# Front weights in 8 KB runs, x fetched turned, and its root applied behind the products

## The chip, the cores and the metric

The kernel runs on one core of one Trainium2 chip. The metric is device time in microseconds (us), lower is better; a time given for a kernel is the median of several executions. The core has TensorE (PE; its weight loads are shown as PEld), VectorE (DVE), ScalarE (ACT), GpSimd (POOL), and SyncE (SP), which issues the transfers from the chip's memory (HBM) to the on-chip buffer (SBUF). TensorE writes its products to a small accumulator memory (PSUM, eight banks).

## The reference

One decoder block on 256 tokens of width 1024. What matters here is its beginning: x is normalised by row and multiplied by w_in; all of z, xbc, dt, q, k, v and the gates come from that one product.

```python
def rms_norm(x, g):
    xf = x.astype(jnp.float32)
    y = xf * lax.rsqrt(jnp.mean(xf * xf, axis=-1, keepdims=True) + EPS)
    return (y * g.astype(jnp.float32)).astype(x.dtype)
...
    n = rms_norm(h, g_mix[i])
    proj = n @ w_in[i]
    z = proj[..., :SPLIT_Z]
    xbc = proj[..., SPLIT_Z:SPLIT_XBC]
    dt_raw = proj[..., SPLIT_XBC:SPLIT_DT]
    ...
    gates = jax.nn.sigmoid(proj[..., SPLIT_V:])
    y_ssd = ssd_mixer(z, xbc, dt_raw, ...) @ w_ssd_out[i]
    y_sb = stick_breaking_attention(q, k, v) @ w_sb_out[i]
    merged = gates[..., :D_MODEL] * y_ssd + gates[..., D_MODEL:] * y_sb
    h = h + merged @ w_out[i]
    h = h + memory_cross_attention(rms_norm(h, g_xattn[i]), rms_norm(mem, g_mem[i]), ...)
    h = h + moe_ffn(rms_norm(h, g_moe[i]), ...)
return rms_norm(h, g_final)
```

The root of a row (the rsqrt) is one number for each token; g_mix is one number for each of the 1024 channels.

## The kernel before

**Two parts.** The front (0 to about 305 us) holds everything up to the router of the mixture of experts; behind it 32 experts follow, whose weights (`w_gu`, `w_down`, 403 MB) are streamed from HBM. All weights pass through one area, `ring`, in SBUF.

**Stripes and chunks.** The front's matrices are cut into stripes of 512 columns (`STRIPES`), and each stripe into chunks of 512 rows by 512 columns, 1 MB each (`CHUNKS`, 42 of them). Stripes 0 to 2 are xbc, then come q, k, v, two of z, four of the gates, and the later matrices. SP fetches the chunks in order into five slots of the ring (L588, a chunk as 128 partitions by four runs of 2 KB) and refills a slot when the low part of the chunk in it has been made.

**Two halves of every number.** A front product is made as three fp32r products: high weight by high x, low weight by high x, high weight by low x. ScalarE rounds a chunk to its high part (`splits_to`, L1487; the first chunk tile by tile in `first_high`, L1525). The low part is weight less high part (`low_part`, L513), four tiles of 128x512 for each chunk: VectorE makes tiles 0 and 1 of chunk 0 and all of chunk 1, GpSimd makes tiles 2 and 3 of chunk 0 and all of chunks 2 and up. There are three buffers of halves (`SPLIT`), so ScalarE can only be three chunks ahead of TensorE. The order of work is written out by hand for each engine; every hand-over is a semaphore.

**The start.** SP fetches x by rows into `h` (L575), seven rows of parameters (L578 to L581), and then the first five chunks. The squares of x are summed by ScalarE (block 0) and VectorE (block 1, L1818), GpSimd takes the root (`root`, L692 and L695), ScalarE (L1493) and VectorE (L1825) scale x, and TensorE turns it with 16 transposes (L889) into PSUM. The parameters are turned into columns `pcol` by another transpose (L902, L1833). From PSUM, x times g_mix is rounded to `xT_hi` (VectorE L1848, ScalarE L1533), and `xT_lo` is the rest (VectorE, L1842). While it waits, TensorE multiplies ones by ones (`ones_products`, L896).

**The first products.** Stripe 0 (`first_products`, L829) takes for each of its two chunks 16 products of high by high, 16 by the low x, and 16 of the low weight. From stripe 1 on (L808) TensorE goes tile by tile and waits for the low part of each tile in the first quarter of a chunk. For xbc, ScalarE applies the last tap of the convolution out of PSUM (L1553) and VectorE adds the other three (L1865); stripe n+2 writes the same banks as stripe n and waits for that. The stripes of q, k, v, z and the gates are emptied by ScalarE (`empty`, L1511), 128x1024 at a time.

**Into the experts.** SP issues the first expert weights as front buffers come free (`EARLY`, `first_free`, `pair_free`), on the same queue behind the chunks.

## Time and profile before

| | us |
|---|---|
| median of 3 runs | 1224.63 (1223.62 to 1225.7) |
| span of the profiled execution | 1222.8 |
| front: first weight product to the router's end | 11.35 to 304 |
| experts and end | 304 to 1222.8 |

The span runs from the first to the last instruction of one execution; the median stands 1.83 us above it. The page of the profile gives the busy time of each engine, the span in 40 slices, the chain of work that ended last, and the costliest groups of instructions. Other views of the trace list instructions in order of time, group them by source line, tell who waited for whom, and give the busy time of each engine in chosen stretches. TensorE's fp32 products count as two instructions in these views; one with fp32r operands as one. Ends of TensorE's instructions are modelled, so starts are read.

### The profile page before, as it was taken

Reading aid. Unit: us, or ns where it says so; the run is one execution under the profiler, and the core shown is the slowest. Engines: PE = TensorE matmul, PEld = TensorE weight load, DVE = VectorE, ACT = ScalarE, POOL = GpSimd, SP = SyncE. Lnnn points to the kernel's source line nnn. Section 1 sums busy time; section 2 is a strip of 40 time slices with the busy share of each in tenths; the row PEclk is TensorE's granted clock in tenths of the full one; section 3 lists DMA queues with packets and bytes.
Section 4 is the critical chain, followed back from the end, with each engine's and each line's share of the span. In section 5 each row is a group of like instructions: output and inputs, shape, how many; then the busy total and the mean of one; then the engine's idle time right before and its main releaser. Section 6 shows DMA issues by size and latency. Waiting matters only on the chain.

```text
span 1222.8 us, 15282 instructions
## 1 busy us (share of the span) xinstructions
PE 1161.0 (95%) x6802; PEld 591.8 (48%) x6802; DVE 302.0 (25%) x463; ACT 245.0 (20%) x349; POOL 235.6 (19%) x206
## 2 busy tenths in 40 slices
PE   9999999999999999999999999989999998899996
PEld 9998878998433333333333333333333333333332
DVE  5448363224311221121122112111211211121112
ACT  6486686445101000000000000000000000000001
POOL 6979769882001000000000000000000000000000
PEclk9999999999999999999999999999999999999999
DMA  9644537848899999999999999999999999999994
GB/s 318 209 138 140 171 104 275 318 154 366 369 426 427 421 429 426 437 430 428 429 429 431 435 431 430 428 433 431 430 430 432 429 431 434 429 429 410 428 427 199
DMA packets 44702, 451.56 MB, mean 369 GB/s; under 512 B 4916, under 2 KB 5272, under 8 KB 27736
## 3 DMA queue, kind: packets, MB, share of 16 engines
q1 hardware_dynamic: 44632, 450.54, 88.8%
q8 instruction: 55, 0.90, 0.3%
q14 instruction: 15, 0.12, 0.0%
HBM read 449.48 MB, written 1.05 MB: 368 GB/s over the span
## 4 chain that ended last, share of the span: by engine, by line
PE 62%; DMA 33%; DVE 2%; ACT 1%; issue 1%; POOL 1%; DVEq 0%; ACTq 0%; POOLq 0%
DMA ring<-in_w_down 20%; PE ps L1275 19%; PE ps L1299 12%; PE ps L865 10%; DMA spare_quad<-in_w_down 7%; DMA kv_quad<-in_w_down 6%; PE ps L808 6%; PE ps L1246 3%; PE ps L1321 2%; PE ps L1178 2%; PE ps L829 1%; PE ps L1312 1%; PE ps L1197 1%; PE ps L980 1%; PE ps L889 0%
## 5 line engine op out<-in xcount | busy, mean ns | idle before, releaser
L513 POOL TENSOR_TENSOR w_parts<-ring,w_parts 128x512 fp32r<-128x512 f32 x162 | 216.9, 1373 | 42.0 <-ACT w_parts L1487 33.3
L692 POOL TENSOR_SCALAR ss<-ss 128x1 f32<-128x1 f32 (+2 forms) x8 | 1.5, 191 | 868.9 <-ACT junk L1477 864.5
L1275 PE MATMUL ps<-ring,xs 128*64 128x512 f32 x688 | 151.8, 595 | 5.8 <-DMA ring<-in_w_gu 5.8
L2216 DVE TENSOR_SCALAR xbuf<-ps 128x512 f32<-128x512 f32 x32 | 22.1, 691 | 526.4 <-PE ps L1275 526.4
L1299 PE MATMUL ps<-ring,xbuf 128*64 128x512 f32 x576 | 128.1, 595 | 17.0 <-DMA ring<-in_w_down 17.0
L1275 PE MATMUL ps<-ring,nT 128*64 128x512 f32 x560 | 123.5, 595 | 3.6 <-DMA ring<-in_w_gu 3.6
L1747 ACT ACTIVATE xbuf<-xbuf 128x512 f32<-128x512 f32 x32 | 20.2, 631 | 469.0 <-DVE xbuf L2216 469.0
L865 PE MATMUL ps<-w_parts,xT_hi 128*128 128x512 f32 x352 | 110.4, 395 | 0.0
L1275 PEld LDWEIGHTS ps<-ring,xs 128*64 128x64 f32 x688 | 47.9, 137 | 101.5 <-issue 90.3
L1487 ACT ACTIVATE w_parts<-ring 128x2048 fp32r<-128x2048 f32 x41 | 78.2, 1915 | 65.3 <-PE ps L865 39.4
L1299 PEld LDWEIGHTS ps<-ring,xbuf 128*64 128x64 f32 x576 | 43.9, 137 | 90.0 <-issue 85.2
L1757 ACT ACTIVATE xbuf<-ps 128x512 f32<-128x512 f32 x31 | 18.5, 597 | 336.5 <-PE ps L1321 336.5
L1275 PEld LDWEIGHTS ps<-ring,nT 128*64 128x64 f32 x560 | 39.2, 137 | 81.0 <-issue 73.9
L865 PEld LDWEIGHTS ps<-w_parts,xT_hi 128*128 128x128 f32 x352 | 65.3, 188 | 14.4 <-issue 0.9
L865 PE MATMUL ps<-w_parts,xT_lo 128*128 128x512 f32 x176 | 68.7, 390 | 0.0
L2232 DVE COPY xbuf<-ps 128x512 f32<-128x512 f32 x32 | 22.1, 691 | 167.7 <-PE ps L1299 167.7
L1246 PE MATMUL ps<-xbuf,scr 64*128 64x512 f32 x248 | 61.6, 615 | 0.8 <-DVE xbuf L2232 0.8
L808 PE MATMUL ps<-xT_hi,w_parts 128*128 128x256 f32 x320 | 57.9, 284 | 0.0
L1299 PE MATMUL ps<-spare_quad,xbuf 128*64 128x512 f32 x224 | 49.9, 595 | 6.7 <-DMA spare_quad<-in_w_down 6.7
L1275 PE MATMUL ps<-spare_quad,nT 128*64 128x512 f32 x240 | 53.2, 595 | 1.8 <-DMA spare_quad<-in_w_gu 1.8
L1275 PE MATMUL ps<-kv_quad,nT 128*64 128x512 f32 x224 | 49.7, 594 | 1.8 <-DMA kv_quad<-in_w_gu 1.8
L808 PEld LDWEIGHTS ps<-xT_hi,w_parts 128*128 128x128 f32 x320 | 49.9, 192 | 0.0
(312 smaller groups left out, 1314.3 us busy)
## 6 DMA issues: line engine op xcount, KB each, us to landing
ring<-in_w_gu SPq DMA_DIRECT2D x24, 4096.0 KB, 41.5
ring<-in_w_gu SPq DMA_DIRECT2D x30, 2048.0 KB, 14.8
ring<-in_w_down SPq DMA_DIRECT2D x12, 4096.0 KB, 39.7
spare_quad<-in_w_gu SPq DMA_DIRECT2D x8, 4096.0 KB, 41.5
kv_quad<-in_w_gu SPq DMA_DIRECT2D x8, 4096.0 KB, 41.6
ring<-in_w_in SPq DMA_DIRECT2D x24, 1024.0 KB, 5.2
ring<-in_w_down SPq DMA_DIRECT2D x12, 2048.0 KB, 14.7
kv_quad<-in_w_gu SPq DMA_DIRECT2D x10, 2048.0 KB, 15.0
```

The lines of the kernel that those rows point to most:

```text
L513: ops.tensor_tensor(w_lo[:, m % SPLIT, c], ring_slot(m)[:, c], w_hi[:, m % SPLIT, c], ALU.subtract).then_inc(lo_ready[name], 1)
L808: i = mm(ps[:, b0 + cb // 2, (cb % 2) * T:(cb % 2 + 1) * T], w[:, k, cb * P:(cb + 1) * P], a[:, 4 * c + k, :], start=(c == 0 and k == 0 an ...
L865: i = mm(ps[:, b0 + b, :], a[:, 4 * c + k, b * P:(b + 1) * P], w[:, k, :], start=(c == 0 and k == 0 and q == 0), stop=(4 * c + k == STRIPE ...
L1178: mm(ps[64 * half:64 * half + 64, 4 + q, :], sel[quadrant(i), e, :], bgu[quadrant(i), :], start=True, stop=False, skip_group_check=True)
L1246: i = mm(ps[:, 2 * b + half, :], hot[r, b, :], yb[r, :], start=False, stop=False, skip_group_check=True)
L1275: i = mm(ps[64 * half:64 * half + 64, 4 + q, :], xg[:, k, (j % GE) * SLOTS:(j % GE + 1) * SLOTS], w[:, q * FF + half * 512:q * FF + half * ...
L1299: i = mm(ps[64 * half:64 * half + 64, 6, :], turned[:, k, :], w[:, k % 4, half * 512:(half + 1) * 512], start=(k == 0), stop=(k == FF // P ...
L1321: i = mm(ps[r, 7, c * 64:(c + 1) * 64], actv[r, c * 64:(c + 1) * 64], ident[r, r], start=True, stop=True)
L1487: af(w_hi[:, m % SPLIT, :], ring_slot(m), ACT.Copy).then_inc(hi_ready, 1)
L1747: af(sg, gl, ACT.Sigmoid, scale=ALPHA).then_inc(sg_ready, 1)
L2216: V.tensor_scalar(gl, ps[:, 4, :], LIM, None, ALU.min).then_inc(gl_ready, 1)
L2232: return V.tensor_copy(yb, ps[:, 6, :])
```

## The change

The host lays the inputs out anew (only copies and transposes, no arithmetic): every chunk lies as 128 rows of 8 KB, one for each partition; x comes twice, by rows and turned (channels on partitions, two halves of 4 KB runs); the parameter columns come ready. On the chip:

- x is not scaled or turned. ScalarE and VectorE round turned x times g_mix out of SBUF (`x_high`, `x_low`), and the products are of x without its root.
- The row copy of x is fetched eighth, behind chunk 2. Its squares are summed as before, ScalarE takes a square root (`root`), VectorE the reciprocal.
- TensorE makes the row of roots behind stripe 0 (`scale_row`): the column of roots, repeated, by the identity, so that each partition holds the root of all 256 tokens. VectorE copies it (`x_scale`).
- VectorE multiplies the xbc stripes in PSUM by that row before ScalarE's tap (`scale_stripe`), and empties q and k with it in place of ScalarE. v, z and the gates are scaled as ScalarE empties them, now in two instructions of 128x512. The step's 16 columns are scaled where their bias is added.
- The halves of `w_dt` are made later, behind stripe 1's taps; GpSimd's product for the router stands a little later.

```diff
-WARM = (18, 8, 4)
+WARM = (20, 4)
...
+            sp_.dma_start(pcol[:], columns).then_inc(prm_in, 16)
+            fetch_x(0)
             for m, (n, c) in enumerate(CHUNKS):
...
+                if m == 0:
+                    half = LO_HALF * SW
+                    halves = chunks[m].rearrange("(a q) (s n) -> a (q s) n", a=2, s=2)
+                    sp_.dma_start(ring_slot(m)[:, 0:half], halves[0]).then_inc(first_in, 16)
+                    sp_.dma_start(ring_slot(m)[:, half:], halves[1]).then_inc(slot_full[slot(m)], 16)
+                    fetch_x(1)
+                else:
+                    sp_.dma_start(ring_slot(m), chunks[m]).then_inc(slot_full[slot(m)], 16)
+                if m == 2:
+                    sp_.dma_start(h[:], x_rows).then_inc(x_in, 16)
...
+            def scale_row():
+                pe.wait_ge(consts, 5)
+                pe.wait_ge(rstd, 1)
+                for b in range(TB):
+                    i = mm(ps[:, 5, b * P:(b + 1) * P], ss[:, b:b + 1].broadcast_to([P, P]), ident[:],
+                           start=True, stop=True)
+                i.then_inc(row_done, 1)
...
             ones_products(WARM[0])
-            pe.wait_ge(prm_in, 16 * 7)
-            pe.wait_ge(consts, 5)
-            nc.tensor.transpose(ps[:, 3, 0:ROWS], prow, ident[0:ROWS, 0:ROWS]).then_inc(pt_done, 1)
-            ones_products(WARM[1])
-            pe.wait_ge(normed_act, 1)
-            pe.wait_ge(normed, NORMED[TR_X])
-            pair_transposes(xn, (0, 1, 2, 3))
-            for n in range(3):
-                stripe(n, xT, tiles=x_lo if n == 0 else None)
+            pe.wait_ge(prm_in, 16)
+            stripe(0, xT)
+            scale_row()
+            stripe(1, xT)
+            stripe(2, xT)
...
+                if name in ("v", "z", "gate"):
+                    act.wait_ge(rstd, 1)
+                    for b in range(TB):
+                        ins = af(dst[:, b], src[:, b], func, scale=ss[:, b:b + 1])
+                    return ins.then_inc(stripe_out["act"], 1)
...
+            x_high((2, 3))
             first_high((0, 1))
             first_high((2, 3))
+            x_high((4, 5, 6, 7))
             splits_to(2)
-            act.wait_ge(dtw_in, 64)
-            af(w_dt_hi[:], w_dt[:], ACT.Copy).then_inc(dt_hi, 1)
+            act.wait_ge(x_in, 16)
+            squares(h[:, 0, :], 0)
+            act.wait_ge(sq_dve, 1)
+            root(0, 2)
             for n in range(3):
                 splits_to(products_done(n) + SPLIT - 2)
                 act.wait_ge(chunk_used, products_done(n))
                 splits_to(products_done(n) + SPLIT - 1)
+                act.wait_ge(x_scaled, n + 1)
...
-            empty(FIRST["q"], scale=DH ** -0.5)
-            empty(FIRST["k"])
+            splits_to(products_done(FIRST["k"]) + SPLIT - 1)
...
+            x_low((0, 1), x_hi_dve, 0)
+            x_low((2, 3), x_hi, 2)
             low_part(dve, V, "dve", 0, tiles=range(LO_HALF))
+            x_low((4, 5, 6, 7), x_hi, 2)
             for m in range(1, LO_DVE):
                 low_part(dve, V, "dve", m)
+            dve.wait_ge(x_in, 16)
+            squares(xn, h, 0)
+            dve.wait_ge(deviation, 1)
+            V.reciprocal(ss[:, 0:2], ss[:, 0:2]).then_inc(rstd, 1)
+            dve.wait_ge(row_done, 1)
+            step(V.tensor_copy(x_scale[:], ps[:, 5, 0:T]))
...
+            def scale_stripe(n):
+                src = channel_stripe(n)
+                V.tensor_tensor(src, src, x_row, ALU.mult).then_inc(x_scaled, 1)
```

What stands in a row on TensorE at the start, before; L896 is the ones, L902 and L889 are transposes, L829 is stripe 0 and L808 stripe 1:

```order
L896 MATMUL ps<-ones 128x128 x18
L902 MATMUL ps<-ident,xbuf 128x100
L896 MATMUL ps<-ones 128x128 x8
L889 MATMUL ps<-ident,xn 128x128 x16
L829 MATMUL ps<-xT_hi,w_parts 128x256 x16
L829 MATMUL ps<-xT_lo,w_parts 128x256 x16
```

And in the changed kernel, where L899 is the ones, L832 stripe 0, L906 the row of roots and L811 stripe 1:

```order
L899 MATMUL ps<-ones 128x128 x20
L832 MATMUL ps<-xT_hi,w_parts 128x256 x16
L832 MATMUL ps<-xT_lo,w_parts 128x256 x16
L832 MATMUL ps<-xT_hi,w_parts 128x256 x32
L832 MATMUL ps<-xT_lo,w_parts 128x256 x16
L832 MATMUL ps<-xT_hi,w_parts 128x256 x16
L906 MATMUL ps<-ident,ss 128x128 x2
L811 MATMUL ps<-xT_hi,w_parts 128x256 x2
```

The transposes are gone, and the two products of the row of roots stand between stripe 0 and stripe 1.

ScalarE at the same place, before; L1477 is the squares, L1493 the scaled x, L1525 and L1487 high parts of weights, L1533 high parts of x, L1544 the half of `w_dt`, L1553 the taps of stripe 0:

```order
L1477 ACTIVATE junk,ss<-h 128x1024
L1493 ACTIVATE xn<-h,ss 128x1024
L1525 ACTIVATE w_parts<-ring 128x512 x2
L1533 ACTIVATE xT_hi<-ps,pcol 128x256 x2
L1525 ACTIVATE w_parts<-ring 128x512 x2
L1533 ACTIVATE xT_hi<-ps,pcol 128x256 x4
L1487 ACTIVATE w_parts<-ring 128x2048 x2
L1544 ACTIVATE w_dt_hi<-w_dt 128x128
L1487 ACTIVATE w_parts<-ring 128x2048 x2
L1553 ACTIVATE xcT<-ps,pcol 128x256 x4
```

And in the changed kernel, where L1549 is the high part of x, L1534 and L1495 those of weights, L1485 the squares, L1525 the square root, L1570 the taps and L1574 the half of `w_dt`:

```order
L1549 ACTIVATE xT_hi<-x_raw,pcol 128x256 x2
L1534 ACTIVATE w_parts<-ring 128x512 x4
L1549 ACTIVATE xT_hi<-x_raw,pcol 128x256 x4
L1495 ACTIVATE w_parts<-ring 128x2048 x2
L1485 ACTIVATE junk,ss<-h 128x1024
L1525 ACTIVATE ss<-ss,eps 128x2
L1495 ACTIVATE w_parts<-ring 128x2048 x2
L1570 ACTIVATE xcT<-ps,pcol 128x256 x4
L1495 ACTIVATE w_parts<-ring 128x2048 x2
L1570 ACTIVATE xcT<-ps,pcol 128x256 x4
L1574 ACTIVATE w_dt_hi<-w_dt 128x128
```

The squares moved from the front of the queue to behind the high parts of chunks 1 and 2, and `w_dt` moved behind stripe 1.

## Rows read from the trace of the kernel before

**Rows 1.** The page: busy time by engine, and GB/s in 40 slices of the span
```profile
PE 1161.0 (95%) x6802; PEld 591.8 (48%) x6802; DVE 302.0 (25%) x463; ACT 245.0 (20%) x349; POOL 235.6 (19%) x206
...
GB/s 318 209 138 140 171 104 275 318 154 366 369 426 427 421 429 426 437 430 428 429 429 431 435 431 430 428 433 431 430 430 432 429 431 434 429 429 410 428 427 199
```

**Rows 2.** Stretches: us, busy of each engine (instructions), TensorE's clock, DMA share, GB/s
```profile
310.00:320.00 10.00, 10.00 (x50) 4.68 (x49) 4.62 (x16) 0.00 (x0) 0.00 (x0) 1.00 0.72 274
...
700.00:800.00 100.00, 92.11 (x550) 35.36 (x548) 16.01 (x24) 5.38 (x11) 0.00 (x0) 1.00 1.00 430
```

**Rows 3.** Waits of PE, 12 to 350 us: us in total, times, longest
```profile
PE ps L1178 <- DVE xbuf L2217: 1.4, 1, 1.4
...
PE ps L1038 <- DVE xcT L1997: 0.6, 1, 0.6
```

**Rows 4.** Waits of SP's queue, 0 to 340 us, same columns
```profile
SPq L588 <- POOL w_parts L513: 209.0, 35, 15.2
SPq L533 <- PE ps L1275: 20.2, 4, 8.7
```

**Rows 5.** The chain, 0 to 300 us: start, us, what
```profile
14.94 8.89 PE ps L829 x72
23.83 23.04 PE ps L808 x192
...
136.28 1.01 ACT gates L1511
...
155.30 5.02 POOL w_parts L513 x4
```

**Rows 6.** TensorE in order of time, 0 to 12 us: start, us, what
```profile
1.20 6.10 PE L896 MATMUL ps<-ones 128*128 128x128 f32 x36 [1.20 <-POOL ones L699]
...
7.33 1.97 PE L896 MATMUL ps<-ones 128*128 128x128 f32 x16
...
11.35 0.84 PE L829 MATMUL ps<-xT_hi,w_parts 128*128 128x256 f32 x5
```

**Rows 7.** SP in order of time: start, us, what
```profile
0.80 0.45 SPq L575 DMA_DIRECT2D h<-in_x  x1
...
3.83 4.61 SPq L588 DMA_DIRECT2D ring<-in_w_in  x5
```

**Rows 8.** Issue to landing: x (L575), chunks 1 and 2, chunks 2 to 4 (L588)
```profile
DMA to landing us min/median/max: 5.2/5.2/5.2
...
DMA to landing us min/median/max: 7.6/8.6/9.7
...
DMA to landing us min/median/max: 9.7/11.9/14.9
```

**Rows 9.** ScalarE in order of time
```profile
12.59 1.56 ACT L1533 ACTIVATE xT_hi<-ps,pcol 128x256 fp32r<-128x256 f32 x4
14.01 3.74 ACT L1487 ACTIVATE w_parts<-ring 128x2048 fp32r<-128x2048 f32 x2
22.53 0.31 ACT L1544 ACTIVATE w_dt_hi<-w_dt 128x128 fp32r<-128x128 f32 x1 [4.78 <-DMA head_rows<-in_d_skip]
```

**Rows 10.** Line 513 in 15 to 24.5 us: ns min/median/max, first and last start
```profile
L513 DVE TENSOR_TENSOR w_parts<-ring,w_parts x3: 675/677/679, 16.8 to 18.0; 128x512 fp32r<-128x512 f32 x3
...
L513 POOL TENSOR_TENSOR w_parts<-ring,w_parts x2: 1292/1901/2510, 17.9 to 20.4; 128x512 fp32r<-128x512 f32 x2
...
L513 POOL TENSOR_TENSOR w_parts<-ring,w_parts x3: 1291/1292/1301, 20.4 to 22.9; 128x512 fp32r<-128x512 f32 x3
```

**Rows 11.** Groups by line: busy us, mean ns, idle before them
```profile
L1511 ACT ACTIVATE gates<-ps 128x1024 f32<-128x1024 f32 x4 | 4.1, 1016 | 0.0
...
L1601 ACT ACTIVATE scr<-ps 128x512 f32<-128x512 f32 x8 | 4.3, 596 | 6.7 <-PE ps L966 6.7
...
L2061 DVE TENSOR_TENSOR ps<-ps,gates 128x1024 f32<-128x1024 f32 x2 | 2.5, 1233 | 10.1 <-PE ps L865 10.1
...
L1818 DVE CUSTOM_DVE_ANT_0 xn<-h 128x1024 f32<-128x1024 f32 x1 | 1.2, 1224 | 6.0 <-DMA h<-in_x 6.0
```

More of the change, by code:

```diff
@@ L465, in build @@
         tr_done = sem("tr_done")
+        xr_in = [sem(f"xr_in{i}") for i in range(2)]
+        first_in, row_done, x_scaled = map(sem, ("first_in", "row_done", "x_scaled"))
         x_hi, x_hi_dve, x_lo, y_hi, y_lo, m_hi, m_lo, h_hi, h_lo = map(
             sem, ("x_hi", "x_hi_dve", "x_lo", "y_hi", "y_lo", "m_hi", "m_lo", "h_hi", "h_lo"))
-        table_in = sem("table_in")
-        pt_done, pcol_ready = sem("pt_done"), sem("pcol_ready")
         tap_out, conv_done, silu_done = sem("tap_out"), sem("conv_done"), sem("silu_done")
@@ L1510, in empty, with root @@
                            "gate": lambda: gates[:, :, i * SW:(i + 1) * SW]}[name]()
+                if name in ("v", "z", "gate"):
[3 more added lines that the diff above has]
+                    return ins.then_inc(stripe_out["act"], 1)
                 return af(dst, src, func, scale=scale).then_inc(stripe_out["act"], 1)
+            def root(c0, cols):
+                act.wait_ge(sq_done, sq[0])
+                s = ss[:, c0:c0 + cols]
+                af(s, s, ACT.Sqrt, bias=eps[:], scale=1.0 / D).then_inc(deviation, 1)
             act.wait_ge(consts, 4)
-            af(rsm[:, 0:4], mhalf[:], ACT.Square).then_inc(table_in, 1)
-            act.wait_ge(table_in, 1)
-            act.wait_ge(x_in, 16)
-            squares(h[:, 0, :], 0)
-            normalise(xn, h, 0, 1)
+            step(af(rsm[:, 0:1], eps[:], ACT.Sqrt, bias=eps[:], scale=1.0 / D))
             def first_high(tiles):
-                act.wait_ge(slot_full[slot(0)], filled(0))
+                act.wait_ge(*((first_in, 16) if tiles[0] < LO_HALF else (slot_full[slot(0)], filled(0))))
                 for k in tiles:
@@ L1554, in _ @@
                        scale=pcol[:, ROW_CW + 3 * NCB + c:ROW_CW + 3 * NCB + c + 1]).then_inc(tap_out, 1)
+                if n == 1:
+                    act.wait_ge(dtw_in, 64)
+                    af(w_dt_hi[:], w_dt[:], ACT.Copy).then_inc(dt_hi, 1)
             act.wait_ge(dt_chan, 1)
@@ L1882, in per_head @@
                 return head_rows[:, i, :].unsqueeze(1).broadcast_to([P, TB, H_SSD])
-            V.tensor_tensor(dt4[:, 0], ps[:, 4, 0:32].rearrange("p (b h) -> p b h", b=TB), per_head(0),
-                            ALU.add).then_inc(dt_raw, 1)
+            for b in range(TB):
+                i = V.scalar_tensor_tensor(out=dt4[:, 0, b], in0=ps[:, 4, b * H_SSD:(b + 1) * H_SSD],
+                                           scalar=ss[:, b:b + 1], in1=head_rows[:, 0, :], op0=ALU.mult, op1=ALU.add)
+            i.then_inc(dt_raw, 1)
             dve.wait_ge(dt_raw, 1)
@@ L2287, in _, with laid_out, by_partition @@
                                        op0=ALU.mult, op1=ALU.mult).then_inc(out_ready, 1)
-_INS = ["x", "mem", "g_mix", "w_in", "conv_w", "conv_b", "dt_bias", "a_log", "d_skip", "g_ssd", "w_ssd_out",
-        "w_sb_out", "w_out", "g_xattn", "g_mem", "w_xq", "w_xkv", "w_xo", "g_moe", "w_router", "b_router",
-        "w_gu", "b_gu", "w_down", "b_down", "g_final"]
+_INS = ["x_rows", "x_turned", "columns", "mem_rows", "chunks", "w_step", "dt_bias", "a_log", "d_skip", "g_moe",
+        "w_router", "b_router", "w_gu", "b_gu", "w_down", "b_down"]
+def laid_out(inputs):
+    def by_partition(rows):
+        return np.asarray(rows).reshape(-1, P, rows.shape[-1]).transpose(1, 0, 2)
+    a = dict(inputs)
+    a["x_rows"], a["mem_rows"] = by_partition(inputs["x"][0]), by_partition(inputs["mem"][0])
+    a["x_turned"] = by_partition(np.asarray(inputs["x"])[0].T).reshape(P, 2, KD // 2, T).transpose(1, 0, 2, 3)
+    rows = [np.asarray(inputs[n]).reshape(-1, P) for n in ("g_mix", "g_xattn", "g_mem", "g_ssd", "conv_w", "conv_b",
+                                                           "g_final")]
+    a["columns"] = np.concatenate(rows).T
+    a["w_step"] = by_partition(np.asarray(inputs["w_in"])[0, :, COL_DT:COL_Q])
+    chunks = []
+    for n, c in CHUNKS:
+        _, mat, col, _, _, _ = STRIPES[n]
+        chunks.append(by_partition(np.asarray(inputs[mat])[0, c * 4 * P:(c + 1) * 4 * P, col:col + SW]).reshape(P, CH))
+    a["chunks"] = np.stack(chunks)
+    a["chunks"][0] = chunks[0].reshape(P, 2, CH // 2).transpose(1, 0, 2).reshape(P, CH)
+    return a
 def kernel(**inputs):
```

124 lines of the change are left out of this document (59 added, 65 removed).

## The prediction

> **What bounds the kernel now.** First the page: TensorE is busy 95% of the span, and GB/s stands near 430 in nearly every slice from the twelfth on [rows 1]. So there are two parts. From about 340 us on, the weights of the experts run without a gap (a DMA share of 1.00 and 430 GB/s in 700 to 800 us, TensorE idle for 8 us in it [rows 2]): the end is the moment at which this stream began, plus its bytes at 430 GB/s. It began when buffers came free, and SP waited for that: 20.2 us in four waits for TensorE [rows 4]; between 310 and 320 us the share is only 0.72 [rows 2]. So an advance of TensorE in the front should move the whole stream forward, one for one.
>
> In the front TensorE is the bound. Its waits between 12 and 350 us that are longest are 1.4 and 0.6 us [rows 3]; the chain runs along its products, 192 of them in 23.04 us, 0.12 us each [rows 5]. The chunks are not late: SP stood 209 us in 35 waits for a slot to come free [rows 4]. What is open is the start, 11.35 us until the first weight product [rows 6], and whatever new wait comes behind it.
>
> **The start.** Before, the first products wait for x, its root, its scaling and the transposes. Now they wait for the ones, turned x, its rounding, and the first half of chunk 0. Ones: 18 products (36 instructions) begin at 1.20 and the next batch at 7.33, 8 products in 1.97 us, 0.25 each [rows 6]. Twenty end at 7.3 + 2 x 0.25 = 7.8. Stripe 0 is 96 products of 0.12, 11.5 us, to 19.3 if nothing is late; the row of roots is two fp32 products of 128 columns like the ones, 0.5 us, to 19.8. Stripe 1 began at 23.83 [rows 5], so this path alone would gain 4.0 us.
>
> **The transfers.** x by rows landed 5.2 us after its issue at 0.80, at 6.0 [rows 7, 8]. The five chunks were issued from 3.83 on, some 0.5 us apart; chunk 1 (at 4.3) landed at 11.9, chunk 2 (4.8) at 14.5, so 1 MB takes about 2.6 us there. In the new order chunk 2 is again the end of the fourth megabyte, behind two halves of x, two of chunk 0, and chunk 1: no later than 14.5 at the old rate. At the rate of the expert stream, 430 GB/s [rows 2], a megabyte takes 2.44 us and it lands at 6.0 + 3 x 2.44 = 13.3, the other bound. I take 13.9, between them, since its runs are 4 and 8 KB, neither the 2 KB of before nor the longer ones of the experts. By the same ladder (2.5 us for 1 MB): turned x first half 5.0, chunk 0 in halves 6.3 and 7.6, x second half 8.9, chunk 1 11.4, x by rows 16.4, chunk 3 18.9, chunk 4 21.4.
>
> **What rides on them.** ScalarE: a tile of x takes 0.39 us (1.56 for four), a chunk's high part 1.87 (3.74 for two) [rows 9]. The first two high tiles of chunk 0 are there by 7.7, in time for TensorE at 7.8; x tiles 4 to 7 at 10.5; chunk 1 at 13.3, needed at 13.6; chunk 2 at 13.9 + 1.9 = 15.8. VectorE's part of chunk 1 is four times 0.68 [rows 10], done at 16.1, needed from 17.6. So stripe 0 runs nearly without a stop.
>
> GpSimd is the tight one. It may begin chunk 2 at 15.8, four tiles at 1.29 us; but one of before took 2.51, the one that began at 17.9 while VectorE was at its own line 513 (until 18.6 + 0.7) [rows 10]. VectorE's squares, 1.22 us [rows 11], read two SBUF operands and fall at 16.4 to 17.6, so I charge half of that collision: 5.2 + 0.6, and GpSimd ends at 21.7 (21.1 without, 22.3 with all of it). TensorE wants the fourth tile of chunk 2 nine products into stripe 1, at 19.8 + 1.1 = 20.9. It stops for 0.8 us. Stripe 1 then ends 87 products later, at 21.7 + 10.4 = 32.1. Before, it ended at 23.83 + 11.52 = 35.35. **Gain 3.25 us.** From chunk 3 on GpSimd makes a chunk in 5.2 us and TensorE uses one in 5.76, and ScalarE no longer stands 4.78 us for the small transfers behind `w_dt` [rows 9]; there the distance grows again.
>
> The Trainium skill speaks against this change here: SBUF — State Buffer, section "Who interferes with whom", says that GpSimd shares a pair of SBUF ports with VectorE under an exclusive lock. The trace agrees with the 2.51 us tile; by the rule alone, with all squares inside GpSimd's chunk, the gain would be 0.6 us less, without it 0.6 more. The low parts of x, now read from SBUF and not PSUM, fall under it as well, but before 12.4 us, when GpSimd has only two tiles to make.
>
> **The root.** x by rows lands at 16.4; squares 1.2, square root and reciprocal some 0.2 each with their hand-overs: the root is there at about 18.3, before TensorE asks at 19.3. Everything on TensorE is queued behind that wait, so each microsecond that the row copy comes after 17.4 is lost whole.
>
> **The scaling.** VectorE gets three products of 128x1024 on PSUM, 1.23 us each (taken from line 2061, which does the same [rows 11]). For stripes 1 and 2 they run while ScalarE makes a high part (1.87), ahead of its taps, and cost nothing; if ScalarE had no such part first, each would cost its 1.23. For stripe 0 they end at 21.5, before ScalarE has made chunk 4 (lands 21.4, 23.3); its convolution ends near 30, and stripe 2 wants that bank at 32.1. q and k leave ScalarE (2 x 1.0) for VectorE, which waits there anyway.
>
> v, z and the gates are emptied by two instructions of 0.60 in place of one of 1.02 [rows 11], 0.2 us more, up to 0.3 with the scale. Seven times, but ScalarE is ahead of TensorE at most of them. Only in the stick-breaking part does a chain pass through it: gates at 136.28, then GpSimd's chunk at 155.30 [rows 5], and at its end TensorE waits 0.6 us on line 1038 [rows 3]. There I charge 0.3 us, between 0 and 0.6 (two of them).
>
> **Sum.** 3.25 - 0.3 = 2.95 us, and the chunks' faster landing later in the front is worth nothing, since slots and not transfers are waited for. The span goes from 1222.8 to 1219.9; the median stands 1.83 above the span, so 1224.63 - 2.95 = 1221.7.
>
> **The rivals.**
>
> *GpSimd in time.* Chunk 2 lands at 13.3 and VectorE's squares miss GpSimd's tiles: 13.3 + 1.9 + 5.3 = 20.5, no stop. Gain 4.0, to 1220.6. For it speaks the stream's rate with long runs; against it that the first transfers start cold.
>
> *Inputs at the old rate.* The longer runs don't speed the first transfers. Chunk 2 at 14.5 and a full collision: 14.5 + 1.9 + 6.4 = 22.8, stripe 1 ends at 33.2, 2.1 gained, 0.3 to 0.6 lost: 1222.9. The row copy would land at 17.1, still in time. This is also the case in which the new layout does nothing.
>
> *The gain stays in the front.* The experts' stream sets its own time from 340 us on; if its start hung on transfers and not on TensorE, the end would stay: 1224.6. For it: 8% of TensorE idle there [rows 2]. Against it: SP's waits for TensorE and the share of 0.72.
>
> *Slower: each transfer pays its fixed time.* The first four megabytes are now eight transfers with the small one, not five. x took 5.2 us, of which 1 MB at 430 GB/s is 2.44, so 2.8 are fixed. If the three added ones paid this in turn, chunk 2 would land 8 us later, stripe 1 end at 40, and the kernel take about 1224.6 - 2.95 + 8 = 1229.7. The point is 1 us each (3 us in all use up the gain). Against it: the chunks issued 0.5 us apart land some 2.6 us apart with 7.6 to 9.7 from issue to landing [rows 8], so they overlap.
>
> **How the numbers follow.** Forecast 47% (1221.7, its own range 1221.0 to 1222.5), GpSimd in time 16% (1220.6), old rate 22% (1222.9), gain left in the front 8% (1224.6), slower 7% (1226 and more). About 0.2%, 2.4 us, is what can be told from no change, so faster is under 1222.2: most of the first, all of the second, a little of the third, 0.57. Same: 0.35; slower: 0.08. The range takes in the best case less half the spread of the runs before (2.1 us), 1219.6, and the old rate and most of the fourth case above: 1224.6.
>
> **What would show it.** Right: first weight product near 7.8, row of roots without a wait near 19.3, stripe 1 from 19.8 with a stop of 0.8 us for GpSimd's line, stripe 2 from about 32.1, the last router product some 3 us before that of now, and the same 430 GB/s behind it. Wrong: a wait of TensorE for the root, a stop inside stripe 0 for chunk 1's high part (it has 0.3 us to spare), a stop of stripe 2 for the convolution, or an expert stream at another rate: 0.3% of 900 us would undo the gain.

## The result and the profile after

The changed kernel takes 1232.03 us (median of 5 executions, 1230.91 to 1233.82), the kernel before, beside it, 1224.09. The ratio is 1.0062, 95% interval [1.0051, 1.0073]: slower by 7.9 us, where 2.9 us less were forecast. The profiled execution is the slowest of its five; its span is 1232.0, 9.2 us above the 1222.8 of before, and the accounts below are made against that one.

The page of the changed kernel, busy time by engine and GB/s in 40 slices, to be read against [rows 1]:

```profile
PE 1163.9 (94%) x6777; PEld 591.0 (48%) x6777; DVE 315.3 (26%) x469; ACT 246.6 (20%) x355; POOL 235.5 (19%) x205
...
GB/s 339 218 100 140 192 115 214 306 172 315 382 430 424 425 427 428 431 431 434 426 434 431 428 434 430 429 431 430 432 429 430 435 427 434 431 425 414 427 427 187
```

The stream of the experts has the rate it had. VectorE has gained 13 us of busy time, far more than the three products of 1.23 us, and the emptying of q and k, that it got. TensorE's waits (us in total, times, longest), 5 to 400 us, show one that is not in [rows 3]:

```profile
PE ps L922 <- POOL identx L725: 8.6, 1, 8.6
...
PE ps L1046 <- DVE xcT L2042: 0.6, 1, 0.6
PE ps L811 <- POOL w_parts L512: 0.6, 1, 0.6
```

Line 922 is the 24 products of `w_dt`. The view names GpSimd's copies to `identx`. They raise a counter (`consts`) that those products wait for too, but the products want 9 of it, and GpSimd has made its ninth before its first tile. What they also wait for is `dt_lo`, the low half of `w_dt`, and that is VectorE's. VectorE in order of time (start, us, what), 40 to 54 us:

```profile
39.73 2.43 DVE L1903 SCALAR_TENSOR_TENSOR xcT<-ps,pcol,xcT 128x254 f32<-128x254 f32 x5
42.07 11.30 DVE L1917 TENSOR_TENSOR w_dt_lo<-w_dt,w_dt_hi 128x128 fp32r<-128x128 f32 x1
53.29 1.22 DVE L1893 TENSOR_TENSOR ps<-ps,x_scale 128x1024 f32<-128x1024 f32 x1
```

GpSimd in the same order, 14 to 54 us:

```profile
16.65 6.01 POOL L512 TENSOR_TENSOR w_parts<-ring,w_parts 128x512 fp32r<-128x512 f32 x4 [4.36 <-ACT w_parts L1495]
23.22 29.95 POOL L512 TENSOR_TENSOR w_parts<-ring,w_parts 128x512 fp32r<-128x512 f32 x24 [0.55 <-ACT w_parts L1495]
53.12 0.39 POOL L725 COPY identx<-ident 32x128 f32<-32x128 f32 x1
```

A subtraction of 128x128 stands in the records as 11.30 us of work on VectorE. It asked at 42.07 and ended at 53.37, 0.2 us after the end of GpSimd's run of 24 tiles without a gap (53.17). GpSimd did not stand still there: its next instruction, a copy, began at 53.12. TensorE was ready for the products at 44.9, 1.9 us ahead of before (46.87, the two chain rows of [rows 5]), and began at 53.5. It then lost a second time. Stretches of the changed kernel (us, busy time of PE, PEld, DVE, ACT, POOL with instructions, granted clock, DMA share, GB/s):

```profile
44.00:46.00 2.00, 0.94 (x8) 0.73 (x7) 2.00 (x1) 0.98 (x1) 2.00 (x3) 1.00 0.69 209
46.00:48.00 2.00, 0.00 (x0) 0.00 (x0) 2.00 (x1) 0.93 (x1) 2.00 (x2) 1.00 0.75 315
48.00:50.00 2.00, 0.00 (x0) 0.00 (x0) 2.00 (x1) 0.00 (x0) 2.00 (x3) 0.59 0.49 70
50.00:52.00 2.00, 0.00 (x0) 0.00 (x0) 2.00 (x1) 0.00 (x0) 2.00 (x3) 0.50 0.93 393
52.00:57.00 5.00, 3.49 (x17) 2.40 (x18) 3.84 (x5) 1.93 (x4) 4.20 (x12) 0.50 0.59 208
57.00:59.00 2.00, 2.00 (x13) 1.51 (x12) 1.89 (x6) 0.20 (x1) 0.00 (x0) 0.60 0.20 78
59.00:61.00 2.00, 2.00 (x20) 2.00 (x18) 1.89 (x5) 0.17 (x1) 0.00 (x0) 1.00 0.00 0
```

The granted clock fell to 0.50 (1.2 of 2.4 GHz) while TensorE stood idle and was still there when the products came. They are three groups of 8; their mean is 0.41 us in the changed kernel:

```profile
L922 PE MATMUL ps<-xT_hi,w_dt_lo 128*16 128x256 f32 x8 | 3.3, 415 | 0.0
L922 PE MATMUL ps<-xT_lo,w_dt_hi 128*16 128x256 f32 x8 | 3.3, 411 | 0.0
L922 PE MATMUL ps<-xT_hi,w_dt_hi 128*16 128x256 f32 x8 | 3.3, 410 | 8.6 <-POOL identx L725 8.6
```

and 0.276 in the kernel before:

```profile
L914 PE MATMUL ps<-xT_hi,w_dt_hi 128*16 128x256 f32 x8 | 2.2, 276 | 0.0
```

From the first of them to the next stripe that makes 5.2 us against 2.7. The account: 1.9 us ahead at 44.9, 8.6 lost in the wait, 2.5 in the clock, so 9.2 behind (64.74 against 55.57 at the second half of the q stripe). The span ends 9.2 behind too, but that the two are equal is chance: on the way 0.3 us are lost at the gates, 1.2 regained at 300 to 310 us, where the clock fell in the kernel before and not here, and 1.0 lost again behind 340 us.

### The profile page after: what moved, and what is told of

It reads as the page before. It is cut to its first block, busy times and chain, and to the rows that moved or that the text cites. A ratio compares the mean times of both kernels' runs of the same rounds, so it can differ in the third digit from the quotient of the medians.

```text
span 1232.0 us, 15241 instructions
## 1 busy us (share of the span) xinstructions
PE 1163.9 (94%) x6777; PEld 591.0 (48%) x6777; DVE 315.3 (26%) x469; ACT 246.6 (20%) x355; POOL 235.5 (19%) x205
## 4 chain that ended last, share of the span: by engine, by line
PE 59%; DMA 34%; POOL 3%; DVE 2%; ACT 1%; issue 1%; SPq 0%; DVEq 0%; ACTq 0%; POOLq 0%
PE ps L1283 19%; DMA ring<-in_w_down 16%; PE ps L1307 12%; PE ps L868 10%; DMA spare_quad<-in_w_down 6%; DMA kv_quad<-in_w_down 6%; PE ps L811 4%; DMA kv_quad<-in_w_gu 3%; PE ps L1254 3%; POOL w_parts L512 3%; PE ps L1329 2%; PE ps L1186 2%; DMA ring<-in_chunks 1%; PE ps L1205 1%; PE ps L1320 1%
## 5 line engine op out<-in xcount | busy, mean ns | idle before, releaser
L1495 ACT ACTIVATE w_parts<-ring 128x2048 fp32r<-128x2048 f32 x41 | 78.4, 1915 | 68.4 <-PE ps L868 39.2
L811 PE MATMUL ps<-xT_hi,w_parts 128*128 128x256 f32 x320 | 58.3, 284 | 0.6 <-POOL w_parts L512 0.6
L811 PEld LDWEIGHTS ps<-xT_hi,w_parts 128*128 128x128 f32 x320 | 49.9, 192 | 1.1 <-POOL w_parts L512 0.8
```

Source lines behind the costliest of these rows:

```text
L811: i = mm(ps[:, b0 + cb // 2, (cb % 2) * T:(cb % 2 + 1) * T], w[:, k, cb * P:(cb + 1) * P], a[:, 4 * c + k, :], start=(c == 0 and k == 0 an ...
L1495: af(w_hi[:, m % SPLIT, :], ring_slot(m), ACT.Copy).then_inc(hi_ready, 1)
```

## The experiments

### Which instruction: four runs

**Theory L**: the low half of `w_dt` on VectorE, with both operands in SBUF, gets no turn while GpSimd's line 512 runs on. The first run takes it off VectorE; its edit to the changed kernel:

```diff
             for m in range(LO_DVE, 9):
                 low_part(pool, nc.gpsimd, "pool", m)
+                if m == 5:
+                    pool.wait_ge(dtw_in, 64)
+                    pool.wait_ge(dt_hi, 1)
+                    nc.gpsimd.tensor_tensor(w_dt_lo[:], w_dt[:], w_dt_hi[:], ALU.subtract).then_inc(dt_lo, 1)
...
-                if c == 7:
-                    dve.wait_ge(dt_hi, 1)
-                    V.tensor_tensor(w_dt_lo[:], w_dt[:], w_dt_hi[:], ALU.subtract).then_inc(dt_lo, 1)
```

> The changed kernel, but the low half of w_dt is made by GpSimd itself, behind the low part of chunk 5, not by VectorE. Theory L (VectorE's instruction with two SBUF operands gets no turn while GpSimd's line 512 runs without a gap, 42.1 to 53.4 us): the 8.6 us wait of TensorE goes, and with it the 2.5 us that its first 24 products behind it took longer at the lower clock; TensorE reaches the w_dt products near 45 us, the time is 1221 to 1223. Rival W (w_dt or its high half lands late): the wait stays, 1232. Rival S (the scaling by VectorE is what costs): 1229 to 1232.

Measured: 1221.60 us against 1224.45, ratio 0.9977 [0.9967, 0.9987], the first version faster than before. GpSimd makes the half in 0.47 us, and TensorE reaches the products at 44.91 without a wait. By tile (ns, start):

```profile
L724 POOL TENSOR_TENSOR w_dt_lo<-w_dt,w_dt_hi x1: 473/473/473, 37.8 to 37.8; 128x128 fp32r<-128x128 f32 x1
```

The second leaves it on VectorE and has GpSimd stop for it:

```diff
+                if m == 7:
+                    pool.wait_ge(dt_lo, 1)
                 low_part(pool, nc.gpsimd, "pool", m)
```

> The changed kernel with one wait added: GpSimd waits for the low half of w_dt before it begins the low part of chunk 7. VectorE's instruction, its place and its operands are as in the changed kernel. Theory L: it ends when GpSimd ends chunk 6 (about 43.5 us), busy for some 1.5 us and not 11.3, and the time is 1221 to 1223. If the instruction is slow for a reason of its own or waits for its data, it still ends near 53 us, GpSimd waits with it, and the time is 1232 or more.

Measured: 1222.20 us, ratio 0.9985 [0.9975, 0.9994]; the half took 0.80 us:

```profile
41.95 0.80 DVE L1919 TENSOR_TENSOR w_dt_lo<-w_dt,w_dt_hi 128x128 fp32r<-128x128 f32 x1
```

The third gives the kernel before nothing but this one move (ScalarE's high half behind stripe 1's taps, VectorE's low half behind its convolution):

```diff
-            dve.wait_ge(dt_hi, 1)
-            V.tensor_tensor(w_dt_lo[:], w_dt[:], w_dt_hi[:], ALU.subtract).then_inc(dt_lo, 1)
...
+                if c == 7:
+                    dve.wait_ge(dt_hi, 1)
+                    V.tensor_tensor(w_dt_lo[:], w_dt[:], w_dt_hi[:], ALU.subtract).then_inc(dt_lo, 1)
```

> The kernel before with this one part of the change: both halves of w_dt are made behind stripe 1's taps and convolutions, nothing else is changed. Theory L: VectorE's instruction begins near 44 us and ends when GpSimd's run ends at 55; TensorE, which asks at 46.9, waits 8 us, and loses up to 2.5 more at the lower clock: 1232 to 1235. If the wait belongs to the new start (scaling, late transfers), this kernel takes 1224.

Measured: 1233.99 us, ratio 1.0083 [1.0066, 1.01]. VectorE there:

```profile
43.88 10.79 DVE L1878 TENSOR_TENSOR w_dt_lo<-w_dt,w_dt_hi 128x128 fp32r<-128x128 f32 x1
```

The fourth puts a copy of `w_dt` into an unused bank of PSUM (ScalarE) and subtracts from there, so that VectorE reads one operand from SBUF; GpSimd runs on:

```diff
+                    af(ps[:, 7, 0:P], w_dt[:].rearrange("p k n -> p (k n)"), ACT.Copy).then_inc(dt_hi, 1)
...
-                    dve.wait_ge(dt_hi, 1)
-                    V.tensor_tensor(w_dt_lo[:], w_dt[:], w_dt_hi[:], ALU.subtract).then_inc(dt_lo, 1)
+                    dve.wait_ge(dt_hi, 2)
+                    V.tensor_tensor(w_dt_lo[:], ps[:, 7, 0:P].rearrange("p (k n) -> p k n", k=KD), w_dt_hi[:],
+                                    ALU.subtract).then_inc(dt_lo, 1)
```

> The changed kernel, but ScalarE also copies w_dt to a free PSUM bank and VectorE takes the first operand from there; order and place stay. Theory L (it is the second SBUF operand that needs GpSimd's turn): the instruction takes some 0.2 to 0.3 us beside GpSimd's run, as the convolution's do (0.48 us for 128x253, one operand in PSUM), and the time is 1221 to 1223. If any VectorE instruction that reads SBUF is held: 11 us and 1232.

Measured: 1222.53 us, ratio 0.9984 [0.9974, 0.9994]:

```profile
42.03 0.28 DVE L1918 TENSOR_TENSOR w_dt_lo<-ps,w_dt_hi 128x128 fp32r<-128x128 f32 x1
```

At the same place and time it takes 0.28 us instead of 11.30. Theory L holds, and the move of this one step carries the whole loss: alone it costs the kernel before 9.5 us, and the change without it is no slower than before.

### The dose, and the clock

GpSimd's pause one chunk later than in the second run (ahead of chunk 8, not 7):

> The changed kernel, with GpSimd waiting for the low half of w_dt ahead of its chunk 8 instead of not at all (the run before paused it ahead of chunk 7 and came to 1222.2). Theory (the low half ends where GpSimd first pauses, wherever that is): it ends at about 48.2, takes some 6 us where it took 11.3 without a pause and 0.80 with the earlier one, TensorE waits some 3.5 us, and the time lies between the two, 1225 to 1227. Rival (the low half is slow for a reason of its own, such as its place in VectorE's row, and the earlier run was quick because GpSimd's chunk 7 came later): it still takes 10 us or more and ends near 53, time 1230 or more.

Measured: 1227.37 us, ratio 1.0025 [1.0014, 1.0035], a little above the range expected; TensorE waited 3.1 us, and the half ended at 48.16, just behind the end of GpSimd's last tile before the pause (48.0):

```profile
42.37 5.79 DVE L1919 TENSOR_TENSOR w_dt_lo<-w_dt,w_dt_hi 128x128 fp32r<-128x128 f32 x1
```

For the clock, TensorE was given products of ones to do in the wait, first 24, then 36 (`ones_products(24, 6)` behind `stripe(2, xT)`):

> The changed kernel, with 24 more products of ones on TensorE behind stripe 2, in the wait for the low half of w_dt; nothing else differs. Theory (the wait is set by VectorE's low half, which gets no turn until GpSimd's run of line 512 ends, and the wait then costs a second time because TensorE's granted clock fell to 0.50 in it): the low half still takes some 11 us and ends at about 53, the ones fill some 6 of the 8.6 us, the 24 products of w_dt take 2.7 us where the changed kernel took 5.24, and the time is 2.5 us less than the changed kernel's 1232.0, about 1229.5. Rival (the clock is no cause, and what came after the wait was late for another reason): the 24 products still take about 5 us, time about 1232.

> The changed kernel with 36 products of ones behind stripe 2 (the run before had 24, and left TensorE idle for 2.6 us). Theory (the fall of the granted clock is the second half of the loss, and an idle stretch of 2.6 us still brought it on): the ones at 0.23 us each fill the whole wait, from about 44.9 to 53.2, the granted clock stays 1.00, the 24 products of w_dt take 2.7 us (5.24 in the changed kernel, 4.35 in the run with 24), time about 1229.5. Rival (the products of w_dt are slow for another reason than the idle time): they still take more than 4 us, time 1231 or more.

With 24 they ended at 50.2, TensorE stood idle for the 2.6 us that were left, and the clock fell all the same; the products took 4.35 us, a miss of the expectation:

```profile
52.00:57.00 5.00, 4.22 (x23) 2.98 (x24) 3.81 (x7) 1.93 (x4) 3.45 (x12) 0.66 0.65 210
```

With 36 there was no idle time and the products took 2.73 us (53.10 to 55.83):

```profile
52.00:57.00 5.00, 5.00 (x45) 4.43 (x44) 3.84 (x6) 2.27 (x5) 3.80 (x12) 1.00 0.59 215
```

So the traces show the 2.5 us to be the clock's. The medians don't resolve it: 1231.43 with 24 and 1230.92 with 36 (4 executions each), 0.6 and 1.1 us under the changed kernel, with intervals of the ratios that overlap; about 1229.5 was expected of both. In the profiled execution with 36 TensorE is 2.8 us ahead of the changed kernel at the second half of q, but only 0.8 at 340 us: at 310 to 320 us its granted clock was 0.69, and 1.00 in the changed kernel.

### The other parts of the change

Long runs alone: the kernel before, its chunks laid out by the host as in the change.

```diff
-                src = mats[mat][c * 4 * P:(c + 1) * 4 * P, col:col + SW]
-                sp_.dma_start(ring_slot(m).rearrange("p (k n) -> p k n", k=4),
-                              src.rearrange("(k p) n -> p k n", p=P)).then_inc(slot_full[slot(m)], 16)
+                sp_.dma_start(ring_slot(m), chunks[m]).then_inc(slot_full[slot(m)], 16)
```

> The kernel before, with only the front's weights laid out in 8 KB runs; x and its root, the order of VectorE, ScalarE and TensorE and the row of roots stay as they were. Theory (the front's transfers are not what the path waits for once the first chunks are in): the time stays within 1.5 us of the kernel before, 1223 to 1225, though the small packets fall to about a fifth. Rival (long runs bring the chunks earlier and the path follows): the first stripes end 1 us or more earlier, and the time is 1222.5 or less. Second rival (the long runs come later, as chunks 3 and 4 did in the changed kernel): 1226 or more.

Measured: 1224.13 us against 1224.46, ratio 1.0001 [0.9992, 1.001]. Packets under 8 KB fall from 27736 to 6232, and nothing follows, as the prediction had it: slots are waited for.

GpSimd's late begin on chunk 2: the first version of above, with four tiles of 128x512 on ScalarE in place of one instruction of 128x2048 for that chunk.

```diff
+                    if m == 2:
+                        for k in range(KT):
+                            c = slice(k * SW, (k + 1) * SW)
+                            af(w_hi[:, m % SPLIT, c], ring_slot(m)[:, c], ACT.Copy).then_inc(hi_ready, 1)
```

> The changed kernel with the low half of w_dt made by GpSimd behind its chunk 5 (the run that came to 1221.6), and with ScalarE rounding chunk 2 in four tiles of 128x512 instead of two of 128x1024, so that GpSimd can begin on the first of them earlier. Theory (stripe 1's stop of about 0.6 us and what follows it is set by GpSimd's late begin on chunk 2): GpSimd begins 0.8 to 1.3 us earlier, the stop goes, and the time falls by 0.3 to 1.0 us below that run, to 1220.6 to 1221.3. Rival (ScalarE's four instructions cost more than the two, and what is gained at chunk 2 is lost at chunks 3 and 4): 1221.6 or more.

Measured: 1221.19 us, ratio 0.9977 [0.9968, 0.9986]: inside the range expected, but not to be told from the 0.9977 without. GpSimd began 1.8 us earlier and the stop for it was gone, but VectorE's squares then took 2.31 us beside it (1.96 without), and TensorE stood for the root instead:

```profile
PE ps L912 <- DVE ss L1891: 0.5, 1, 0.5
```

### Why this instruction and no other

Elsewhere in the same traces VectorE instructions with two SBUF operands met GpSimd's line 512 and had their turn at the end of the tile. So what is special here? Three runs of the changed kernel, with one line each ahead of the low half: a wait for the end of the tap before it; a wait for the end of stripe 2; a 128x512 subtraction of two pieces of x.

```diff
+                    dve.wait_ge(conv_done, 8)
...
+                    dve.wait_ge(chunk_used, products_done(2))
...
+                    V.tensor_tensor(xn[:, 0, 0:SW], h[:, 0, 0:SW], h[:, 0, SW:2 * SW], ALU.subtract)
```

> The changed kernel, with one more wait on VectorE: the low half of w_dt starts only when the tap before it has ended (before, the two overlap by 0.08 us); GpSimd's run is left alone. Everywhere else in the traces a VectorE instruction with two SBUF operands that came upon GpSimd's line 512 got its turn at the next end of a tile, 1.3 us at most; this one alone passed nine ends. Theory B (it is passed over because it follows an instruction of another kind without a gap): it gets its turn at the next end, takes at most 1.6 us, TensorE waits not at all, time about 1222. Theory S (it is passed over for its shape, 128x128): it still takes about 11 us, time about 1232.

> The changed kernel, with VectorE waiting ahead of the low half of w_dt until TensorE has done stripe 2, so that it stands idle for over 2 us before it (the run sent beside this one gives it only the end of its predecessor); GpSimd's run is left alone. Theory B (passed over because it follows another instruction closely): it begins at about 45, has its turn at the next end of a tile, ends by 46.6, TensorE waits up to 1.7 us, time 1223 to 1225. Theory S (passed over for its shape): it begins at about 45 and ends at about 53, TensorE waits over 8 us, time about 1232.

> The changed kernel, with one more VectorE instruction, a difference of two SBUF halves of x (128x512, its result is used by nobody), between the tap and the low half of w_dt. Theory B (what follows the tap closely is passed over, whatever its shape): the added instruction takes some 11 us and the low half 0.3 us behind it, time about 1232. Theory S (the shape 128x128 is what is passed over): the added one takes at most 2 us, as others of its shape did beside GpSimd, and the low half follows within it or stalls for 9 us.

Measured: 1231.97, 1232.56 and 1232.75 us. VectorE in the first, the second and the third:

```profile
41.82 10.55 DVE L1918 TENSOR_TENSOR w_dt_lo<-w_dt,w_dt_hi 128x128 fp32r<-128x128 f32 x1
```

```profile
45.35 7.76 DVE L1918 TENSOR_TENSOR w_dt_lo<-w_dt,w_dt_hi 128x128 fp32r<-128x128 f32 x1 [2.82 <-PE ps L811]
```

```profile
42.60 11.73 DVE L1916 TENSOR_TENSOR xn<-h 128x512 f32<-128x512 f32 x1
54.26 0.37 DVE L1918 TENSOR_TENSOR w_dt_lo<-w_dt,w_dt_hi 128x128 fp32r<-128x128 f32 x1
```

Whatever came, after whatever, stood until GpSimd's run was over. Theories B (its predecessor) and S (its shape) both fall.

**Theory R**: it is how long GpSimd has run without standing still. Three more runs: two such 128x512 subtractions as probes in the version with PSUM (behind the second block of stripe 0 and of stripe 1); a pause of GpSimd ahead of chunk 5; both halves of `w_dt` one stripe earlier.

```diff
+                if c in (1, 5):
+                    V.tensor_tensor(xn[:, 0, 0:SW], h[:, 0, 0:SW], h[:, 0, SW:2 * SW], ALU.subtract)
...
+                if m == 5:
+                    pool.wait_ge(x_scaled, 2)
...
-                if c == 7:
+                if c == 3:
```

> The version with the first operand of the low half of w_dt in PSUM (1222.5 us), with two more VectorE instructions of two SBUF halves of x (128x512, results used by nobody): one behind the second block of taps of stripe 0, near 29.5 us, some 5 tiles into GpSimd's unbroken run, the other behind the second block of stripe 1, near 39, some 12 tiles in. Theory R (VectorE gets its turn early in a run of GpSimd, and no more once the run is long): the first takes at most 2 us, the second stalls until GpSimd next stands still, near 53, and the time is 1230 or more. Theory T (only the stretch behind stripe 1 is bad, for something that happens there): both take at most 2 us, time 1222 to 1224. If already the first stalls, so that the convolution comes 20 us late, neither holds, and then what matters lies before 29.5 us.

> The changed kernel, with GpSimd waiting ahead of its chunk 5 for VectorE's product over stripe 1 (34.7 us), some 1.4 us of standstill in the middle of its run; the low half of w_dt then comes upon a run of 6 tiles and not of 15. Theory R (the length of the run decides): it gets its turn at the next end of a tile and takes at most 1.6 us, TensorE does not wait for it, time 1222 to 1223.5. Theory T (the place decides): it takes about 11 us, time about 1232.

> The changed kernel, with both halves of w_dt one stripe earlier: the high one on ScalarE behind the taps of stripe 0 (27.5 us), the low one on VectorE behind the convolution of stripe 0 (32.4 us, 7 tiles into GpSimd's run). Theory R (early in a run VectorE gets its turn; elsewhere it did so 7 tiles in): the low half takes at most 1.6 us, TensorE does not wait for it, time 1222 to 1223. Theory T: the same. Theory W (in this run of GpSimd VectorE is passed over wherever it asks): it stalls from 32.4 on, the products over stripe 1 and with them the taps come some 20 us late, TensorE waits for the bank, time 1236 or more.

The probes both had their turn (1222.29 us in one execution). The second was 12 tiles into the run, where theory R said it would stand. So from here on the theory is another: a turn given to VectorE counts like a standstill, and the first probe had been given one between; the distance from that is 9.2 us.

```profile
29.49 0.69 DVE L1917 TENSOR_TENSOR xn<-h 128x512 f32<-128x512 f32 x1
...
39.33 1.36 DVE L1917 TENSOR_TENSOR xn<-h 128x512 f32<-128x512 f32 x1
```

With the early pause the low half took 0.41 us (1223.27 us, ratio 0.9992 [0.9982, 1.0002]). GpSimd and VectorE there:

```profile
34.18 20.14 POOL L512 TENSOR_TENSOR w_parts<-ring,w_parts 128x512 fp32r<-128x512 f32 x16 [2.08 <-DVE ps L1895]
```

```profile
41.48 0.41 DVE L1919 TENSOR_TENSOR w_dt_lo<-w_dt,w_dt_hi 128x128 fp32r<-128x128 f32 x1
```

One stripe earlier it stood in the profiled execution (1227.26 us), where 1.6 us at most were expected, and the ten executions lie between 1220.52 and 1229.15 (median 1223.85, ratio 0.9996 [0.998, 1.0012]):

```profile
31.23 11.84 DVE L1917 TENSOR_TENSOR w_dt_lo<-w_dt,w_dt_hi 128x128 fp32r<-128x128 f32 x1
```

The last two put the distance to the test: the changed kernel with GpSimd's pause ten tiles ahead of the low half, and the version one stripe earlier with the pause two tiles ahead (`pool.wait_ge(conv_done, 2)` ahead of chunk 4 in both).

> The changed kernel, with GpSimd's standstill one chunk earlier than in the run with the early pause: it waits ahead of chunk 4 for the second block of stripe 0's taps (29 us), so that the low half of w_dt (42 us) comes upon its tenth tile since then, not its sixth. Theory R (VectorE gets its turn only within the first tiles of a run: where it did, GpSimd was at most 7 tiles from its last standstill or hand-over; where it did not, at least 9): it stalls until 54 all the same, some 11 us, time 1230 or more. Rival (any standstill of GpSimd since stripe 0 is enough): at most 1.6 us, time 1222 to 1224.

> The version with both halves of w_dt behind stripe 0, whose profiled execution stalled 11.8 us (its low half came upon the ninth tile or so since the last hand-over) and whose times lay between 1220.5 and 1229.2, with GpSimd waiting ahead of chunk 4 for the second block of stripe 0's taps (29 us): the low half at 31.3 then comes upon the second or third tile. Theory R: it takes at most 1.6 us, the spread is gone, time 1221 to 1222.5. Rival (early in the kernel VectorE is passed over wherever the tile count stands): it stalls again, time 1225 or more in some executions.

With two tiles it had its turn in the profiled execution, 1.27 us for the low half, and by the times it never stood: 1222.47 us (1220.86 to 1224.74), ratio 0.9981 [0.9972, 0.9991]. With ten tiles, where theory R had it stand, the ten executions fall into two groups, four of 1221.4 to 1223.8 us and six of 1231.4 to 1234.4 (median 1232.06). The profiled one was of the first group, against the theory:

```profile
42.23 1.46 DVE L1919 TENSOR_TENSOR w_dt_lo<-w_dt,w_dt_hi 128x128 fp32r<-128x128 f32 x1
```

All cases by the time between the end of GpSimd's last standstill, or of the VectorE instruction that last had a turn, and VectorE's asking (from the rows above and those of the same views):

| us | case | outcome |
|---|---|---|
| 2.7 | pause two tiles ahead, one stripe earlier | turn, 1.27 us |
| 6.2 | first probe | turn, 0.69 |
| 7.3 | early pause | turn, 0.41 |
| 8.6 | line 1981 of the changed kernel, at 92.0 | turn, 1.30 |
| 9.2 | second probe | turn, 1.36 |
| 12.0 | one stripe earlier | stands 11.8 in the one profiled; times from 1220.5 to 1229.2 |
| 12.6 | pause ten tiles ahead | turn, 1.46, in the one profiled; by their times 6 of 10 stand |
| 18.8 | changed kernel; wide probe | stands 11.3; 11.7 |
| 23.0 to 25.9 | kernel before with `w_dt` late; GpSimd pausing late; ones in the wait; tap ended; stripe 2 ended | stands to the end of the run, each time |

Within some 9 us the turn came at the next end of a tile; from some 19 on it never did; at 12 to 13 one of the two that were profiled stood and the other did not. Theory R, as changed by the probes, agrees with this order, but it was fitted to most of these rows, and it does not say why times of one kernel fall apart. Part of that may be the distance itself, which is known for the profiled executions alone: the changed kernel's GpSimd stood still for 0.55 us at 23 us, and in the profiled execution with the wait for the tap, the same program up to there, it ran through. Whether time or tiles count, and what in the chip counts them, is open.

## Why the prediction was wrong, point by point

**The step that failed** is in the part on GpSimd: "and ScalarE no longer stands 4.78 us for the small transfers behind `w_dt` [rows 9]; there the distance grows again." The moved step was two instructions and I costed one. VectorE's low half went from 22.87 us, where it took 1.44 us and GpSimd stopped at 24.16 for want of a chunk, into the middle of 24 tiles without a stop. It had no term in the sum, no rival and no place in the range. It cost 8.6 us, and 2.5 behind it for the clock. VectorE and GpSimd before, rows that the prediction does not use:

```profile
16.76 2.48 DVE L513 TENSOR_TENSOR w_parts<-ring,w_parts 128x512 fp32r<-128x512 f32 x4
22.87 1.44 DVE L1874 TENSOR_TENSOR w_dt_lo<-w_dt,w_dt_hi 128x128 fp32r<-128x128 f32 x1 [3.63 <-ACT w_dt_hi L1544]
...
17.89 6.27 POOL L513 TENSOR_TENSOR w_parts<-ring,w_parts 128x512 fp32r<-128x512 f32 x4 [2.25 <-ACT w_parts L1487]
24.78 30.18 POOL L513 TENSOR_TENSOR w_parts<-ring,w_parts 128x512 fp32r<-128x512 f32 x24 [0.62 <-ACT w_parts L1487]
```

**The bound that was misread.** I took the 2.51 us tile of [rows 10] as a collision worth at most one tile, and its half as the price. It is a wait to the end of the other engine's run: VectorE had two tiles left when it asked at 17.89, they ended at 19.24, and GpSimd's first tile came behind them. Read so, the question would have been how long the other runs on, here 11 us. The Trainium skill (SBUF — State Buffer, "Summary: rules for kernel authors") says that when a VectorE instruction with two SBUF inputs meets a GpSimd instruction that reads SBUF, the second to issue blocks until the first finishes. Turns at the end of a tile, as line 1981's, agree with that; nine ends of tiles passed in a row go beyond it, and there the runs decide.

**The rest of the sum**, which the first version (low half on GpSimd) shows without the failed step: 1221.6 us, where 1221.7 was forecast. That is partly luck. At the products of `w_dt` it is 1.8 us ahead of before (45.07 against 46.87 in the two chains), where 3.25 were forecast at the end of stripe 1. Its chain shows the terms that were sized too small:

```profile
3.64 11.07 DMA ring<-in_chunks
14.73 1.93 ACT w_parts L1499
16.79 6.02 POOL w_parts L512 x4
22.86 22.21 PE ps L815 x183
```

Chunk 2 lands at 14.7 (13.9 forecast) and GpSimd ends it at 22.8 (21.7; by its own terms, 15.8 + 5.2 + 0.6, the forecast should have read 21.6), so 1.1 of the 1.45 us that are missing lie ahead of TensorE's first product behind that chunk. Term by term in the changed kernel, TensorE in order of time:

```profile
1.20 7.67 PE L899 MATMUL ps<-ones 128*128 128x128 f32 x40 [1.20 <-POOL ones L703]
8.63 2.15 PE L832 MATMUL ps<-xT_hi,w_parts 128*128 128x256 f32 x16
...
20.21 0.60 PE L906 MATMUL ps<-ident,ss 128*128 128x128 f32 x4
20.58 0.48 PE L811 MATMUL ps<-xT_hi,w_parts 128*128 128x256 f32 x2
```

First weight product at 8.63 (7.8 forecast; 7.3 to 8.5 in the later runs of it), since the ones went slower: in 5 to 7 us TensorE did 11 of their instructions, 0.42 us each, where the kernel before did 19 of 0.28; row of roots without a wait (root ready at 19.57, 18.3 forecast); stripe 1 at 20.58 (19.8). Issue to landing of the row copy of x, issued at 4.21:

```profile
DMA to landing us min/median/max: 12.8/12.8/12.8
```

so 17.0 (16.4 forecast); chunk 2 at 14.6, which is the bound for the old rate (14.5), not 13.9; chunk 3 at 21.1 (4.70 and 16.38 in the chain of waits; 18.9). The rival "inputs at the old rate" was the right one for the transfers, and its 2.1 us of gain in the front are nearest to the 1.8. GpSimd's chunk 2 took 6.01 us with VectorE's squares in it, as charged, from 16.65 (15.8); the stop was 0.63 (0.8). The emptying in two instructions cost 0.3 us, as charged.

The version then regains about 1 us that nobody forecast: at 300 to 310 us TensorE's clock is 1.00 in its profiled execution,

```profile
300.00:310.00 10.00, 8.83 (x60) 6.70 (x61) 5.45 (x20) 8.01 (x13) 3.10 (x3) 1.00 0.97 394
```

where it is 0.83 in the same stretch of before:

```profile
300.00:310.00 10.00, 9.00 (x59) 6.80 (x59) 4.68 (x20) 9.48 (x14) 3.09 (x3) 0.83 0.96 403
```

At 309.4 us it is 2.6 us ahead, and 2.85 in the median. The traces do not tie that clock to the change: of the eight versions of the changed kernel whose low half had its turn in the profiled execution within 1.5 us, or was made elsewhere, four have 1.00 there and four 0.66 to 0.83.

**What held**: an advance of the front moves the stream, which keeps its rate, to within 1 us (the first version is 2.6 us ahead at 309.4 us and 1.8 at the end of its profiled execution, the changed kernel 8.3 behind at 340 us and 9.2 at the end), the packet size is worth nothing, the root is in time, the products over the stripes cost nothing at 1.23 us each, and no transfer paid its fixed time in turn. The rival on the slower side had the right sign and the wrong mechanism.

## What to carry to other kernels

When a step moves, list every instruction of it on every engine, and for each one with two SBUF operands on VectorE look at what GpSimd does in that stretch: a run of its tensor instructions that has gone on for 12 us or more can be a wall, from 19 us on it was one each time, and the price is what is left of the run. Three cheap ways round it worked: make the small thing on GpSimd itself (0.47 us), give VectorE one operand from PSUM (0.28 us, and a copy by ScalarE), or have GpSimd stand still shortly before it. An instruction that shows as busy far beyond its size is a wait, and the engine that a view names as releaser can be one that merely came next.

## What was not expected of the hardware

- A VectorE instruction with two SBUF operands was passed over at nine ends of GpSimd's tiles in a row (11.3 us for 128x128), and whether it is goes with how long GpSimd has run since it last stood still or gave a turn: never within 9.2 us, by the times in 6 of 10 executions of the kernel whose profiled one had 12.6 us, always in what was seen from 18.8 us on.
- While VectorE stands so, its row shows as work (11.30 us busy), and TensorE's wait can be put down to GpSimd's next instruction.
- In the kernel with 24 ones TensorE stood idle for 2.6 us and its granted clock was 0.66 over the 5 us from 52 on, which hold the work behind it; with 36 ones and no idle time it stayed 1.00.
